# Four recurrence heads written out: each head's output and norm moved into the next head's first slot, weight halves made on ScalarE and VectorE, output projection by rows

## What is computed

```python
z = h @ w_in                                    # 1024 -> 7 * 512
bg, cg, xv, qp, fp, ip, gp = split(z)
conv_y = short_conv(cg * xv)                    # 3 taps over time
a_out = bg * conv_y
q = silu(qp) * 128**-0.5;  k = sigmoid(-fp);  logf = log(sigmoid(fp));  v = ip
# 4 heads of 128 x 128 state, chunks of 64 tokens:
o = (q * exp(G)) @ S  +  tril(q k decay) @ v    # G: running sum of logf in the chunk
S = exp(G_last) * S + (k * exp(G_last - G)).T @ v
o = rmsnorm(o, gnorm) * silu(gp)                # norm over a head's 128 channels
y = concat(a_out, b_out) @ w_out                # output projection, 1024 -> 1024
x = x + gate * y
```

## Time and profile before

| | |
|---|---|
| time, median of 3 runs | 3367.51 us (3363.97 to 3367.75) |
| the profiled execution | 3368.71 us, span 3367.1 us |
| PE busy | 3024.3 us, 90% of the span |
| DVE busy | 1052.6 us, 31% |
| POOL busy | 1162.0 us, 35% |
| mean granted clock of PE | 0.948 of full speed |
| recurrence heads and the start of the projection | 96.3 to 773.9 us: 677.6 us, PE busy 541.4 |

### The profile page before, as it was taken

One profiled execution on the slowest core, in us unless ns is written; L12 is line 12 of the kernel. 1 busy time (PEld: TensorE's weight loads), 2 busy tenths in 40 slices (PEclk: granted clock), 3 DMA queues, 4 the chain that ended last, 5 costly groups with the idle time before them and its releaser, 6 DMA issues.

```text
span 3367.1 us, 57103 instructions
## 1 busy us (share of the span) xinstructions
PE 3024.3 (90%) x20941; PEld 2700.1 (80%) x20941; DVE 1052.6 (31%) x2152; ACT 630.0 (19%) x1434; POOL 1162.0 (35%) x1149
## 2 busy tenths in 40 slices
PE   4788888769799999999989999999987999999996
PEld 2677777658699999999977575757666999999996
DVE  1566555631301102020234444444443010111104
ACT  3301101011410010101143323232334101001012
POOL 2411111133533333333564332322326434333343
PEclk7898898889899999999988999999998999999998
DMA  6211011015331431111112222213141111111111
GB/s 215 88 33 32 27 32 39 26 72 161 106 120 50 126 108 47 44 46 48 44 52 89 85 69 69 81 58 90 52 124 36 44 46 50 41 51 41 49 41 66
DMA packets 314587, 226.88 MB, mean 67 GB/s; under 512 B 19235, under 2 KB 306838, under 8 KB 314150
## 3 DMA queue, kind: packets, MB, share of 16 engines
q1 hardware_dynamic: 296902, 204.29, 20.1%
q10 hardware_dynamic: 9312, 11.83, 1.0%
q0 software_dynamic: 8192, 8.40, 0.9%
HBM read 212.30 MB, written 12.17 MB: 67 GB/s over the span
## 4 chain that ended last, share of the span: by engine, by line
PE 79%; DVE 6%; ACT 5%; issue 5%; POOL 2%; DMA 1%; SPq 0%; ACTq 0%; DVEq 0%; POOLq 0%; PEldq 0%
PE bank L1891 20%; PE bank L1892 20%; PE bank L1893 20%; PE bank L2337 2%; PE bank L2336 2%; PE bank L2375 2%; PE bank L2280 2%; PE bank L2259 2%; PE bank L1961 1%; ACT hh L864 1%; ACT htmp L865 1%; PE bank L2065 1%; PE bank L2037 1%; PE bank L2301 1%; POOL hl L672 1%
## 5 line engine op out<-in xcount | busy, mean ns | idle before, releaser
L1891 PE MATMUL bank<-hh,whi 128*128 128x344 f32 (+1 forms) x3468 | 1163.2, 335 | 143.6 <-DVE hq L1352 34.6
L1892 PE MATMUL bank<-hl,whi 128*128 128x344 f32 (+1 forms) x3468 | 1129.8, 326 | 1.2 <-issue 1.2
L1893 PE MATMUL bank<-hh,wlo 128*128 128x344 f32 (+1 forms) x3468 | 1127.4, 325 | 0.0
L1891 PEld LDWEIGHTS bank<-hh,whi 128*128 128x128 f32 x3468 | 671.1, 194 | 192.3 <-issue 149.4
L660 POOL CAST whi<-wst 128x1024 fp32r<-128x1024 f32 (+4 forms) x250 | 211.8, 847 | 1557.8 <-PE bank L1893 1234.1
L1892 PEld LDWEIGHTS bank<-hl,whi 128*128 128x128 f32 x3468 | 670.6, 193 | 9.2 <-issue 8.0
L1893 PEld LDWEIGHTS bank<-hh,wlo 128*128 128x128 f32 x3468 | 669.3, 193 | 0.6
L662 POOL TENSOR_TENSOR wlo<-wst,whi 128x1024 fp32r<-128x1024 f32 (+4 forms) x250 | 468.8, 1875 | 20.1
L1564 DVE TENSOR_TENSOR atmp<-sil,bank 128x344 f32<-128x344 f32 x132 | 67.6, 512 | 962.7 <-PE bank L1893 955.7
L1891 PE MATMUL bank<-ahi,whi 128*128 128x344 f32 x1056 | 338.3, 320 | 0.0
L1892 PE MATMUL bank<-alo,whi 128*128 128x344 f32 x1056 | 337.4, 320 | 0.0
(11 more groups left out here) (293 smaller groups left out, 3023.3 us busy)
## 6 DMA issues: line engine op xcount, KB each, us to landing
adaw<-in_w_ada SPq DMA_DIRECT2D x48, 1024.0 KB, 5.3
wst<-in_w_gu SPq DMA_DIRECT2D x88, 512.0 KB
pk<-in_cache_ckv SPq DMA_DIRECT2D x256, 128.0 KB, 2.4
wst<-in_w_in_even SPq DMA_DIRECT2D x28, 512.0 KB
wst<-in_w_down SPq DMA_DIRECT2D x32, 384.0 KB
wst<-in_w_down SPq DMA_DIRECT2D x32, 320.0 KB
pr<-in_cache_krope POOLq DMA_DIRECT2D x256, 32.0 KB, 2.1
x_rest<-xT ACTq DMA_DIRECT2D x1, 4128.0 KB, 11.2
```

Source lines behind the costliest of these rows:

```text
L1891: mm(out, wh_, xh_, start=start, stop=False)
L1892: mm(out, wh_, xl_, start=False, stop=False)
L1893: return mm(out, wl_, xh_, start=False, stop=stop)
```

## The change

- The loop over pairs of heads becomes four heads written out, on all engines; addresses by register become constants.
- `outputs` and `head_sums` of head h - 1 move into head h: PE runs `outputs_of(h - 1)` behind F chunk 0 and `head_sums(h - 1)` behind F chunk 1. For heads 1 to 3 the order of the first parts becomes F, F, F, Q, Q, Q (it was F, F, Q, F, Q, Q; head 0 keeps that).
- The three sums go to banks 7, 6 and 5, and their squares and roots to `hsq`, three buffers, one for each chunk. ACT's `head_norm(h - 1)` and DVE's `head_tail(h - 1)` stand ahead of head h's evacuations and decay products.
- The mixer's weight halves go from POOL to ACT (`split_high`, a copy of 128x1024) and DVE (`split_low`, a subtraction of 128x1024), seven of each per head, at fixed places of the order.
- DVE's order: the Q evacuations (`query`) between the decay products, `chunk_products` after the first two `product`, the convolution's, sample's and states' steps interleaved otherwise, `dg` ahead of the masking.
- PE's small steps: each `attend` one place later, `sample_values` and the four `outer` one place later, the last `outer` behind G chunk 2.
- Output projection: ACT casts rows 0 to 6 of a chunk within the last head's slot G (`first_rows`), PE multiplies rows 0 to 6 of the three chunks first, with `outputs_of(3)` and `head_sums(3)` between them, and then row 7, the last head's. The residual returns in three transfers (rows 0 and 1, 2 to 6, 7), each with its own wait, and the first pair of slots is written out ahead of the loop.

```diff
 # SP
-                sp.wait_ge(lo_ready, HI_FFN0)
-                sp.dma_start(xT[:], x_rest).then_inc(x_back, 16)
+                for p, (k0, k1_) in enumerate(X_PARTS):          # (0, 2), (2, 7), (7, 8)
+                    sp.wait_ge(lo_ready, HI_OUT + ROWS0 * (NC - 1) + k1_ if k1_ < KT else HI_FFN0)
+                    sp.dma_start(xT[:, k0:k1_, :], x_rest[:, k0:k1_, :]).then_inc(x_back[p], 16)
 # POOL
-            def mixer():
-                with nc.gpsimd.Fori(0, HEADS // 2) as i:
-                    for u in range(14):
-                        split_at(G_IN + 2, i, u, KT, 14)
 # ACT
+            def split_high(g):
+                b = g % 2
+                act.wait_ge(w_loaded[b], 32 * (g // 2 + 1))
+                act.wait_ge(bank_ready[NC - 1], g + 1)
+                nc.scalar.copy(whi[b][:], wst[b][:]).then_inc(w_hi, 1)
+            def head_norm(h):
+                act.wait_ge(oacc_ready, h + 1)
+                for c in range(NC):
+                    nc.scalar.activation(hsq[c], oacc[:, cols(c)], ACT.Square).then_inc(hsq_ready, 1)
+                def root_of(c, src):
+                    nc.scalar.activation(hsq[c], src[:, 0:CW], ACT.Sqrt, bias=EPS, scale=1.0 / P).then_inc(hrt_ready, 1)
+                    act.wait_ge(hrt_ready, NC * h + c + 1)
+                for c in range(2):
+                    b = 1 - c
+                    act.wait_ge(bc_ready[b], BC[b] * h + BC[b])
+                    root_of(c, bank[6 + b])
+                    act.sem_inc(bc_free[b], 1)
+                act.wait_ge(wk_ready, WK * h + 8 + 1)
+                root_of(2, bank[5])
+                act.sem_inc(wk_free, 1)
             def mixer():
+                    if h > 0:
+                        head_norm(h - 1)
                     ...                          # F evacuated
+                    split_high(s + 2)
                     ...                          # Q, split_high(s + 3); V, split_high(s + 4); CG
+                    split_high(s + 5)
+                    split_high(s + 6)
                     tokens(2, ktok[:, 0:4, :])
                     tokens(3, ktok[:, 4:8, :])
+                    split_high(s + 7)
                     ...                          # G
+                        if h == HEADS - 1:
+                            first_rows(c)
+                    split_high(s + 8)
 # DVE
+            def head_tail(h):
+                dve.wait_ge(o_ready, h + 1)
+                ...                              # two sums into oacc, then oacc_ready
+                for c in range(NC):
+                    dve.wait_ge(hrt_ready, NC * h + c + 1)
+                    order(v.reciprocal(rs[:], hsq[c]))
+                    dve.wait_ge(bank_free[c], G_IN + 7 * h + SLOT_G + 2)
+                    order(v.scalar_tensor_tensor(oacc[:, cols(c)], oacc[:, cols(c)], gnT, rs[:], ALU.mult, ALU.mult))
+                    y = xT[:, h + HEADS, cols(c)]
+                    v.tensor_tensor(y, y, oacc[:, cols(c)], ALU.mult).then_inc(y_ready, 1)
             def head(h):
                 order.put(v.memset(ki[0][:], 0.0))
                 order(v.memset(ki[1][:], 0.0))
+                if h > 0:
+                    head_tail(h - 1)
                 for c in range(NC):
                     evacuated(SLOT_F, c)
+                split_low(s + 2)
                     ...                          # decay products, t = 1 to 7
+                    if t % 2 == 1 and t < 2 * NC:
+                        query(t // 2)
                 ...
                 gated_conv(0)
                 ...                              # s0 times forget gate
+                gated_conv(1)
                 sample_states(0)
                 sample_states(1)
                 dve.sem_inc(s_new, 1)
-                gated_conv(1)
+                gated_conv(2)
                 states(0)
-                gated_conv(2)
+                split_low(s + 7)
+                out_gate(0)
                 states(1)
 # PE
-                         (SLOT_BG, 1): [lambda: transposes(3, ki[0]), lambda: outer(0)],
-                         (SLOT_BG, 2): [lambda: outer(1)],
-                         (SLOT_G, 0): [lambda: outer(2), sample_outputs],
-                         (SLOT_G, 1): [lambda: outer(3)],
-                         (SLOT_G, 2): [outputs, lambda: head_sums(0), lambda: head_sums(1), lambda: head_sums(2)]}
+                         (SLOT_BG, 1): [lambda: transposes(3, ki[0]), lambda: sample_values(0), lambda: sample_values(1)],
+                         (SLOT_BG, 2): [lambda: outer(0)],
+                         (SLOT_G, 0): [lambda: outer(1), sample_outputs],
+                         (SLOT_G, 1): [lambda: outer(2)],
+                         (SLOT_G, 2): [lambda: outer(3)]}
+                if h > 0:
+                    steps[SLOT_F, 0] = [lambda: outputs_of(h - 1)]
+                    steps[SLOT_F, 1] = [lambda: head_sums(h - 1)]
             def out_proj():
+                for c in range(NC):
+                    pe.wait_ge(bank_free[c], G_OUT + 1)
+                    for k in range(ROWS0):       # 7 rows
+                        ...
+                    if c == 0:
+                        outputs_of(HEADS - 1)
+                    elif c == 1:
+                        head_sums(HEADS - 1)
+                for c in range(NC):              # row 7
+                    pe.wait_ge(lo_ready, HI_OUT + ROWS0 * NC + c + 1)
+                    ...
```

More of the change, by code:

```diff
@@ L157, in enter, with enter_from @@
         self.base, self.n = i * per + self.start, 0
+    def enter_from(self, i, per, first):
+        self.start, self.per = self.base + self.n, per
+        self.base, self.n = i * per + (self.start - first * per), 0
     def leave(self, turns):
@@ L474, in mixer @@
                 win = w_in_even[0].rearrange("(k p) (z j m) -> p k z j m", p=P, z=7, m=P)
[L475 to L485, removed]
+                for h in range(HEADS):
+                    for u in range(7):
+                        g = G_IN + 7 * h + u
+                        load(g, g % 2, wst[g % 2][:], win[:, :, Z_ORDER[u], h, :])
+                        if u == 4:
+                            sp.wait_ge(so_saved, 16 * h + 16)
+                            sp.dma_start(s0[:], state_hgrn[0, :, h].rearrange("n k v -> k n v")).then_inc(s0_loaded, 16)
             def out_proj():
@@ L1455, in head @@
                 for n in range(0, 12, 2):
+                    for j in (n, n + 1):
+                        dve.wait_ge(bc_ready[j % 2], BC[j % 2] * h + j // 2 + 1)
+                        if j + 2 < 12:
+                            product(j + 2)
+                        weigh(j)
                     keys(n // 2 + 3)
@@ L1551, in ffn, with residual_slots @@
+            def residual_slots(g, gate_at, l, first=0):
+                with nc.vector.Fori(first, KT // 2) as i:
+                    if first == 0:
+                        order.enter(i, 4)
+                    else:
+                        order.enter_from(i, 4, first)
+                    residual_pair(g, gate_at, l, i)
+                    order.leave(KT // 2 - first)
             def ffn(l, g0, inst, ht0, hi0):
@@ L1871, in _ @@
             dve.sem_inc(o_taken, 1)
-            dve.sem_inc(hrs_ready, 1)
             dve.sem_inc(fill_out, 1)
@@ L2124, in head @@
-                g, b = 14 * i + G_IN + 7 * e, e
-                ready = model_lows_ready(HI_MIX, 0)
-                for u, c in ((0, 0), (0, 1), (1, 0), (0, 2), (1, 1), (1, 2)):
-                    part(g + u, (b + u) % 2, c, KT, hh, hl, ready_k=ready if u == 0 else None)
-                for u in range(2, 7):
-                    def after(c):
-                        for step in steps.get((u, c), ()):
-                            step()
-                    slot(g + u, (b + u) % 2, KT, hh, hl, None, after)
@@ new lines, in head @@
+                if h > 0:
+                    steps[SLOT_F, 0] = [lambda: outputs_of(h - 1)]
+                    steps[SLOT_F, 1] = [lambda: head_sums(h - 1)]
+                    first = [(u, c) for u in range(2) for c in range(NC)]
+                else:
+                    first = [(0, 0), (0, 1), (1, 0), (0, 2), (1, 1), (1, 2)]
+                ready = model_lows_ready(HI_MIX, 0) if h == 0 else None
+                for u, c in first + [(u, c) for u in range(2, 7) for c in range(NC)]:
+                    part(s + u, (s + u) % 2, c, KT, hh, hl, ready_k=ready if u == 0 else None)
+                    for step in steps.get((u, c), ()):
+                        step()
```

341 lines of the change are left out of this document (164 added, 177 removed).

## The result

| | before | after |
|---|---|---|
| time, median of the runs timed together | 3367.1 us | 3194.31 us (3191.8 to 3197.72, 4 runs) |
| ratio | | 0.9489, 95% interval 0.9473 to 0.9506 |
| the same, timed again later | 3367.4 us | 3195.5 us (3187.2 to 3198.9, 5 runs), ratio 0.9481 (0.9466 to 0.9495) |
| the profiled execution | 3368.71 us, span 3367.1 | 3191.8 us, span 3190.2 |
| end of the projection's fourth part | 773.9 us | 608.2 us |

The change saves 172.8 us, 5.1%.

A forecast was written before the change was run, and what follows sets the result against it. A chain passing from TensorE to VectorE and back was taken to bound each head. Shorter heads and projection save 156.8 us, 26 in the projection; less 8 allowed, 149, giving 3219 us, range 3203 to 3260.

The forecast's parts named there:

- each wait of rows 3: PE's waits in one head: query product before slot V 8.6 us, keys 5.7, squares 5.4, sample values 4.3, loop turn 2.3.
- the table switch: Rival, chance 0.06: ScalarE's table load before freed bank 0 costs 2.8 us more plus low clock, heads 1 to 3; 3235 us.
- the starved written-out code: Rival, chance 0.03: fetch gaps in straight code make PE wait, slower than before; 3384 us at 35 times.
- the projection that gives little: Rival, chance 0.06: residual transfers or last row's chain in the output projection come 10 to 26 us later; 3229 to 3245.
- I allow 2 us for each head, 8 in all.: Allowance over four heads for some fifty inexact hand-overs between engines, cutting the saving from 156.8 to 149 us.
- VectorE late: Rival, chance 0.22: VectorE work before V0 and `outer(1)` 4 us longer, 10 us a head in three heads; 3249 us.
- The layout of a head, 118.2 us.: New order laid out in time from slot F to the last `outer`: a head takes 118.2 us where it was 153.8.
- PE's floor of 117 us: A head with PE never waiting: 82 us of parts beside small steps plus some 35 us of small steps.
- Granted clock 1.00 through the heads: Expected sign in the profile after: PE at full clock through the heads, where a recurrence head had 0.88.
- The projection, 45.5 us.: Output projection from head 3's last `outer` to the fourth part's end: 45.5 us, ending at 617.1; 26 us saved there.
- Behind 773.9 nothing changes.: Everything after the projection's fourth part, which ended at 773.9 us before, was to take the same time.
- one case with 0.03: Chance 0.03 of a saving above 164 us: PE at 117 us a head, no low clock in the projection; 3204 us.

The follow-up runs named there:

- old_proj: Kernel after with the output projection as before: chunk by chunk, all casts behind the last head, residual in one transfer; 3227.8 us, ratio 0.959.
- dve_late3: Kernel after with three extra VectorE products of 128x1024 ahead of each head's decay products; 3194.8 us.
- the three undone parts: Kernel after with one part undone each time: weight halves back on GpSimd, head tails at own head's end, old output projection; 21, 35 and 33 us lost.
- pool_split: Kernel after with the mixer's weight halves made by GpSimd (POOL) again; 3215.8 us, ratio 0.9553.

## Why the prediction missed, step by step

**Right.** What bounded the kernel, and that each wait of rows 3 would go: the 8.6, 5.7, 5.4, 4.3 and 2.3 us are gone, with no long wait in their place. The prices: subtraction 1.22 us for 1.23, copy 1.05 for at most 1.2, table load 1.28 with no drain, DVE 85.3 us a head for about 88. The rivals of the table switch, the starved written-out code and the projection that gives little didn't happen. In the projection the old order takes 79.0 us from the last `outer` to the end of the fourth part (564.2 to 643.2) and the new one 43.0: 36 us, where the prediction counted 26 (its own numbers, 73.2 less 45.5, give 27.7) and the expectation of `old_proj` 29; undoing it cost 33 us of time.

**Wrong.** Four steps, 25 us together:

- *"I allow 2 us for each head, 8 in all."* None of it was needed: 8.0 us. No row stood behind this term. The chance of trouble at the hand-overs was already the rival VectorE late, with 0.22; the allowance counted it a second time in the likeliest case. `dve_late3` shows that even 1.4 us of waiting in each head left the time where it was.
- *The layout of a head, 118.2 us.* Measured 117.7, 116.1 and 116.2, so 4.6 us in three heads, and 1.8 in head 0 (next head's F at 215.2, not 217.0). Without the 5.7 us of clock falls in the parts, which the layout didn't have, the periods are 114.8 on average. The terms that were too large: the three sums 1.5 us and not 2.2, sample values 1.3 and not 2, a part beside small steps 3.9 and not 3.96, and the waits of 0.4 at Q0 and 0.8 at `outer(1)`, neither of which came. So PE's floor of 117 us was 2.2 too high. "Granted clock 1.00 through the heads" was wrong by 5.7 us the other way.
- *The projection, 45.5 us.* Measured 43.0: 2.5 us, 1.3 of them in the first gap.
- *"Behind 773.9 nothing changes."* True of the work, but the number was taken from one execution, whose 2593.2 us for this stretch are the longest of the three profiled of that kernel (2587.2 the shortest). The kernel after shows 2582.1 and 2588.6, on average 7.9 us less than was booked. Of these, 3.1 us are the first profile of before against the mean of its three (2590.1); the other 4.8 are the difference between the kernels' means, for which no cause is shown. A single profile's rest is not known to better than some 6 us, and the forecast treated it as exact.

8.0 + 6.4 + 2.5 + 7.9 = 24.8 us, and 3219 less 3194.3 is 24.7. That it closes to a tenth is luck, since the last term alone is uncertain by several microseconds. The range failed for the same reason: its lower end, 3203, came from one case with 0.03, PE at 117 us a head, though the allowance, a floor counted with rounded-up terms and the untouched stretch at its longest all leaned to the same side. Without the allowance alone the forecast would have been 3211.

**Open.** What decides in one execution whether the clock falls behind a wait of 1.67 us; which of the runs of one-column matmuls lower it (heads 1 to 3 in both executions of the kernel after, head 0 in `dve_late3`, none, two or two of the four in the kernel before); what took away the 8.6 us ahead of V0; and how the 84 us that the three undone parts leave are shared between the step order, the loop and the parts' joint effect.

## What to carry to other kernels

Put a chain that passes between engines (outputs, sum, root, reciprocal) under the next block's independent products, and measure the reserve with a few dummy instructions: here it was 2.3 us on VectorE ahead of V0. The first 1.4 us of waiting a head beyond it cost 0.3, and at 5.1 us of waiting each microsecond cost 1.45 (29.8 for 20.5), both up to the fourth part of one profiled execution. Don't add an allowance for mishaps to the likeliest case when they already stand as a rival with a chance; and before a stretch is called unchanged, ask how much it moves between executions of one kernel, by profiling the kernel before more than once. Don't issue a run of one-column matmuls in one block in a stretch bound by PE: spread between large ones the same sixteen saved 6 us in three heads.

## What the runs showed of the hardware that was not expected

- The granted clock fell to its lower level of 1.2 GHz with no recorded wait ahead of it, behind sixteen matmuls of one column (24 matmuls in 6.72, 5.57 and 5.55 us instead of 4.01); in three groups of six, six and four it stayed at 1.00. The same run without a fall exists too (4.01 and 4.02 us behind it), so it is not sufficient by itself, and in the kernel before it came in none, two and two of the four heads in three executions.
- VectorE instructions are held up while GpSimd works on two SBUF tiles: a step of 0.58 us took 2.75 as GpSimd's subtraction of 2.38 us ran (`pool_split`), while that subtraction itself costs 1.22 us on VectorE.
- The same 1.67 us wait at the same place of the same kernel was followed by clock 1.00 in one execution and 0.70 in another. One unchanged stage took 533 to 542 us over the profiled executions.
- 5.6 us of added waits left the time where it was (3194.8 against 3194.3 us, medians of 4 runs each). In the one execution profiled, two fewer falls of the clock made up for most of them.
